# Two-layer hybrid encoder trunk: where the high and low parts of the expert weights are staged

## The chip, the cores and the metric

One NeuronCore of a Trainium2 chip runs the whole program. The time is the device time of one execution in microseconds (us); lower is better. The engines are TensorE (PE; its weight loads are listed as PEld and overlap matmuls), VectorE (DVE), ScalarE (ACT), GpSimd (POOL) and SyncE (SP), which issues the weight transfers. Each engine works through its own instructions in the order written; engines wait for each other on counting semaphores.

## The reference

The input is a sequence of 256 tokens of width 1024 in float32. Layer 0 is an input projection, dilated attention beside an RWKV-7 mixer, an output projection and a dense SwiGLU. Layer 1 is a short convolution beside a gated DeltaNet, and then eight experts of which each token uses two. The change touches only the experts:

```python
def moe_swiglu(h, router, w_gate, w_up, w_down):
    ...
    for e in range(N_EXPERTS):
        out = out + gates[..., e:e + 1] * swiglu(h, w_gate[e], w_up[e], w_down[e])
    return out
```

with `swiglu(h, g, u, d) = (silu(h @ g) * (h @ u)) @ d`, N_EXPERTS = 8, and a hidden width of 3584 per expert.

## The kernel before, in words

**Precision.** A float32 product a*w is made of three products of a faster format: a = a_high + a_low, w = w_high + w_low, and a_high*w_high + a_high*w_low + a_low*w_high is summed in one PSUM bank. `product` (L2844) issues these three matmuls, at L2847, L2848 and L2849. The high part of the weights is a rounded copy made by ScalarE (L1204), the low part is weights minus high part, made by VectorE (L2031).

**Weight halves.** Each expert has 7 chunks of 512 hidden columns. A chunk has a gate, an up and a down part, each cut into two halves of [128, 2048] float32 (1 MB). One expert so has PER = 42 halves, in the order of `expert_chunks`: gate j, up j, then down j-1 (the down part of a chunk comes one chunk late). This text numbers the halves of an expert from 0 to 41, chunk j's gate being 6j-2 and 6j-1, its up 6j and 6j+1, then down j-1 at 6j+2 and 6j+3 (chunk 0, with no down part ahead, has 0 and 1, 2 and 3); down 5 is 38 and 39, down 6 is 40 and 41. Halves of the next expert count on from 42. Where b is used, it is the first gate half of a chunk, b+1 the second.

**Path of a half.** SyncE loads it into the ring (tile `ring`, 7 places of one half, L563). ScalarE waits for the landing and for a free staging, and writes the high part into `split`. VectorE waits for the high part and writes the low part beside it. There are NSTAGE = 3 stagings of one high and one low half each, all in the tile `split`. TensorE waits for the low part (w_lo), does the 12 matmuls of the half and counts half_ps. ScalarE waits for half_ps of half r-3 before it writes the high part of half r. SyncE waits for the low part of half r before it loads half r+7 into the same place (L568, L575, L580).

**Duties.** Between the halves, ScalarE and VectorE also do the other work of the experts. It is written into a table by hand, `duties[r]`, and done at step r, ahead of the part of half r:
- silu of chunk j (ScalarE, L1189), at step g1+3, g1 being the second gate half;
- product of chunk j, silu times up (VectorE, L2015), at step u1+3, u1 being the second up half;
- turned: TensorE transposes the product of chunk j behind the gate halves of chunk j+1 (L2906, `turn`), ScalarE copies the result as a high part (L1192) and VectorE makes the low part (L2019), at step g1+3 of chunk j+1; for chunk 6 at step 41;
- tokens (step 40): TensorE transposes the next expert's tokens behind half 37 (L2872, `turn_rows`), VectorE weighs them (L1984, two operations); tokens_split (step 41): ScalarE (L1170) and VectorE (L1993) split them into high and low;
- result of the expert before (step 2): ScalarE scales its two banks (L1156), when half 41 is done; gates (5), select (6) and rows (10) are small.

At the end of an expert TensorE does: up 6 (halves 36, 37), `turn_rows`, half 38, `turn(6)`, half 39, halves 40 and 41. The last expert has no tokens duties. Expert 0 and expert 7 are written out, experts 1 to 6 are one loop.

**Elsewhere.** The dense stage of layer 0 has the same splitting with the low part written over the ring (L1675). GpSimd moves token rows through HBM: copies of x and of the normalised x in the first expert, then one gather and one scatter with addition per expert (L704, L708).

Of the kernel before, what the change touches and what calls it, by code (L numbers as in the profile page):

```python
# [5 lines left out]
F32 = mybir.dt.float32  # L6
F32R = mybir.dt.float32r
# [4 lines left out]
ADD, SUB, MUL, MAX, MIN = ALU.add, ALU.subtract, ALU.mult, ALU.max, ALU.min  # L12

P = 128
D = 1024
SEQ = 256
TT = SEQ // P
KT = D // P
# [6 lines left out]
NE = 8  # L25
# [8 lines left out]
NSTAT = 3  # L34
HALF = 2048
NHALF = 7
NSTAGE = 3
EC = 512
NC_E = FE // EC
NLEV = 7  # L40
# [57 lines left out]
def hybrid_trunk(nc, A, out):  # L98
# [6 lines left out]
    for i, (kind, n, dmas) in enumerate(chunks):  # L105
        s = (i if i < 8 else i + 2) % NSTAT
# [11 lines left out]
    with ctx:  # L118
        def sb(name, shape, dt=F32):
            return ctx.enter_context(nc.sbuf_tensor(name, shape, dt))  # L120
# [45 lines left out]
        alog_row, dt_row = rows[:, BC_AL:BC_AL + 8], rows[:, BC_DT:BC_DT + 8]  # L166


        with nc.sbuf_tensor("scr", [P, NSTAGE * 2 * HALF + KT * SEQ], F32) as scr:
            pass  # L170
        split = sb("split", [P, NSTAGE * 2 * HALF + KT * SEQ], F32R)
        with nc.sbuf_tensor("ehf", [P, 2 * 2 * 4 * P], F32) as ehf:
            pass
        ehr_ = sb("ehr_", [P, 2 * 2 * 4 * P], F32R)
        wst = split[:, 0:NSTAGE * 2 * HALF].rearrange("p (b t n) -> p b t n", b=NSTAGE, t=2)
        xgs = split[:, NSTAGE * 2 * HALF:NSTAGE * 2 * HALF + KT * SEQ].rearrange("p (t k s) -> p t k s", t=2, k=KT)
        ehs = ehr_[:, :].rearrange("p (b t k s) -> p b t k s", b=2, t=2, k=4)
        hT = scr[:, NSTAGE * 2 * HALF:NSTAGE * 2 * HALF + KT * SEQ].rearrange("p (k s) -> p k s", k=KT)

        B = [ctx.enter_context(nc.psum_tensor(f"bank{i}", [P, 512], F32)) for i in range(8)]  # L180

# [101 lines left out]
        Tc2, Pc2, Xs2 = xn_f[:, 0:512], xn_f[:, 512:1024], xn_f[:, 1024:1152]  # L283
        g_o3 = Region(arena, 6144, 4096)
        INVB = [(Tm, Pm, Xm, Am)] * 4 + [tuple([g_o3.take(4, P) for _ in range(2)] for _ in range(4))] * 2
        g_o4 = Region(scr, SCR0, NSTAGE * 2 * HALF)
        yTo, ktok, vto, osum = g_o4.take(KT, SEQ), g_o4.take(TT, 512), g_o4.take(TT, 512), g_o4.take(TT, 512)
        kkm = [g_o4.take(4, P) for _ in range(TT)]
        kqm = [g_o4.take(4, P) for _ in range(TT)]
# [186 lines left out]
        duties[10].append(("rows", 0))  # L476
        for j in range(NC_E):
            g1, u1 = at_half["gate", j, 1], at_half["up", j, 1]
            duties[g1 + 3].append(("silu", j))
            duties[u1 + 3].append(("product", j))  # L480
            duties[at_half["gate", j + 1, 1] + 3 if j + 1 < NC_E else PER - 1].append(("turned", j))
        duties[PER - 2].append(("tokens", 0))
        duties[PER - 1].append(("tokens_split", 0))

# [11 lines left out]

        def used_half(i, ps, r):

            return i * PER + (NE * PER * ps + NSTAGE + r + 1)

        block = ctx.enter_context(nc.Block())

# [2 lines left out]
        def _(sp):  # L505
# [49 lines left out]
            if UPTO >= 4:  # L555
                packed_w = {"gate": A["od_moe_gate"], "up": A["od_moe_up"], "down": A["od_moe_down"]}

                def expert_load(e, r):

                    kind, j, h = order[r]  # L560
                    v = ring[:, (r % NHALF) * HALF:(r % NHALF + 1) * HALF]
                    src = packed_w[kind][e, 2 * j + h].rearrange("o p n -> p (o n)")
                    sp.dma_start(v, src).then_inc(landed_e[r % NHALF], 16)  # L563

                def expert_pass(ps):
                    for r in range(NHALF):
                        if ps:
                            sp.wait_ge(w_lo, NE * PER * ps - NHALF + r + 1)  # L568
                        elif r < 2 * NSTAT:
                            sp.wait_ge(*used_up(*before[r // 2]))  # L570
                        expert_load(slice(0, 1), r)
                    with sp.Fori(0, NE - 1) as i:
                        for r in range(NHALF, PER + NHALF):

                            sp.wait_ge(w_lo, i * PER + (NE * PER * ps + r - NHALF + 1))  # L575
                            if order[r % PER][1:] == (0, 0):
                                sp.sem_inc(sp_pace, 1)
                            expert_load(bass.ds(i + 1 if r >= PER else i, 1), r % PER)
                    for r in range(NHALF, PER):
                        sp.wait_ge(w_lo, (NE - 1) * PER + NE * PER * ps + r - NHALF + 1)  # L580
                        expert_load(slice(NE - 1, NE), r)

                def store(ps):

                    for q in range(4):
                        c = slice(512 * (q // 2), 512 * (q // 2) + 512)
                        sp.wait_ge(cmb_sb, 4 * ps + 1 + q)
                        sp.dma_start(out[0, P * (q % 2):P * (q % 2) + P, c], x_sb[:, q % 2, c]).then_inc(stored, 16)

                expert_pass(0)  # L590
                store(0)
                sp.wait_ge(flag_rdy, 1)
                with sp.If(sp.value_load(flag[0:1, 0:1], min_val=0, max_val=1) > 0):
                    sp.wait_ge(stored, 64)
                    expert_pass(1)
                    store(1)
                    sp.wait_ge(stored, 128)
                sp.wait_ge(stored, 64)
# [132 lines left out]
        def _(act):  # L731
# [382 lines left out]
            if UPTO >= 4:  # L1114
# [57 lines left out]
                def expert(ps, i, at, last_one=False):  # L1172

                    first = at == 0

                    def duty(what, j):
                        if what == "tokens_split":
                            if not last_one:
                                split_tokens(ps, i, at + 1)
                        elif what == "result":  # L1180
                            if not first:
                                result(ps, i, at)
                        elif what == "gates":
                            if last_one:
                                act.wait_ge(st_ps, ps + 1)
                                act.activation(selT, B[3][:, 0:TT * P], ACT.Copy).then_inc(st_sb, 1)
                        elif what == "silu":
                            act.wait_ge(half_ps, used_half(i, ps, at * PER + at_half["gate", j, 1]))
                            act.activation(esil[:, j % 2, :], B[j % 2][:, :], ACT.Silu).then_inc(eg_act, 1)  # L1189
                        elif what == "turned":  # L1190
                            act.wait_ge(ht_ps, i * NC_E + (NC_E * (at + NE * ps) + 1 + j))
                            act.activation(ehs[:, j % 2, 0], B[6 + j % 2][:, :].rearrange("p (k s) -> p k s", k=4),  # L1192
                                           ACT.Copy).then_inc(ht_hi, 1)

                    for r in range(PER + 1):
                        if first and r == 2:
                            split_tokens(ps, 0, 0)
                        for what, j in duties[r]:
                            duty(what, j)
                        if r < PER:  # L1200
                            act.wait_ge(landed_e[r % NHALF], i * (16 * PER // NHALF) + (
                                16 * PER // NHALF * (at + NE * ps) + 16 * (r // NHALF + 1)))
                            act.wait_ge(half_ps, used_half(i, ps, at * PER + r - NSTAGE))
                            act.activation(wst[:, r % NSTAGE, 0, :], ring[:, (r % NHALF) * HALF:(r % NHALF + 1) * HALF],  # L1204
                                           ACT.Copy).then_inc(w_hi, 1)

                def all_experts(ps):
# [14 lines left out]
        def _(dve):  # L1222
# [679 lines left out]
            if UPTO >= 4:  # L1902
# [92 lines left out]
                def expert(ps, i, at, last_one=False):  # L1995
# [26 lines left out]
                    for r in range(PER + 1):  # L2022
                        if at == 0 and r == 2:
                            weigh_tokens(ps, 0, 0)
                            split_tokens(ps, 0, 0)
                            next_rows(ps, 0, 0)
                        for what, j in duties[r]:
                            duty(what, j)
                        if r < PER:
                            dve.wait_ge(w_hi, i * PER + (PER * (at + NE * ps) + r + 1))  # L2030
                            dve.tensor_tensor(wst[:, r % NSTAGE, 1, :], ring[:, (r % NHALF) * HALF:(r % NHALF + 1) * HALF],  # L2031
                                              wst[:, r % NSTAGE, 0, :].bitcast(F32), SUB).then_inc(w_lo, 1)

                def all_experts(ps):

# [24 lines left out]
        def _(pe):  # L2060
# [769 lines left out]
            if UPTO >= 4:  # L2830

                logits(1).then_inc(pe_step, 1)
                pe.sem_inc(half_ps, NSTAGE)
                unread(512)
                unread(256)
                pe.wait_ge(dve_step, DVE_STEPS["as_rdy"])
# [6 lines left out]

                def product(o, hi, lo, r, cols_, start, stop):  # L2844

                    wh, wl = (wst[:, r % NSTAGE, t, cols_] for t in range(2))
                    pe.matmul(o, hi, wh, start=start, stop=False)  # L2847
                    pe.matmul(o, hi, wl, start=False, stop=False)  # L2848
                    return pe.matmul(o, lo, wh, start=False, stop=stop)  # L2849
# [170 lines left out]
```

## Time and profile before

| | |
|---|---|
| median of 3 runs | 1660.81 us (1660.61 to 1662.0) |
| span of the profiled execution | 1664.3 us |
| TensorE busy | 1636.6 us (98%) |
| VectorE busy | 1229.1 us (74%) |
| ScalarE busy | 986.1 us (59%) |
| expert stage, first to last matmul of a half | 686.3 to 1655.5 us |
| transfers over the span | 440.40 MB, mean 265 GB/s |

The profile is of one execution, by the hardware's profiler. A matmul's duration is longer than the distance to the next one, because they are pipelined; the start times tell how fast TensorE goes. "Idle before" an instruction is time in which its engine did nothing, with what ended it in brackets.

### The profile page before, as it was taken

How to read it: one execution, taken by the hardware profiler on the slowest of the kernel's cores; microseconds unless marked ns; L12 is line 12 of the kernel's file. 1: busy time of each engine (PE TensorE's matmuls, PEld its weight loads, DVE VectorE, ACT ScalarE, POOL GpSimd, SP SyncE). 2: the span in 40 equal slices, each digit the busy share in tenths (PEclk: the TensorE clock that was granted, in tenths of full speed). 3: DMA queues.
4: the chain of work that ended last, by engine and by line, in shares of the span. 5: the costliest groups of instructions: out<-in, count | busy, mean ns of one | idle time of the engine just before them, and what ended most of it. 6: DMA issues, size and time to landing. Idle time of an engine off the chain costs nothing.

```text
span 1664.3 us, 21926 instructions
## 1 busy us (share of the span) xinstructions
PE 1636.6 (98%) x8446; PEld 1343.7 (81%) x8446; DVE 1229.1 (74%) x1203; ACT 986.1 (59%) x955; POOL 101.0 (6%) x122
## 2 busy tenths in 40 slices
PE   8999999999999999999999999999999999999997
PEld 4868995999988886788788788788888888888886
DVE  5578545444424673788888988988888888988886
ACT  3356333434334422677777777777777777777774
POOL 2005230000000030010000000000000000000000
PEclk9999999999999999899999999999999999999999
DMA  6311014455444211899999999999999999999993
GB/s 248 109 62 40 1 52 152 152 198 169 165 153 150 103 51 39 315 421 412 355 375 383 361 381 376 367 382 367 375 376 358 390 371 363 390 367 350 410 375 122
DMA packets 102340, 440.40 MB, mean 265 GB/s; under 512 B 11114, under 2 KB 34942, under 8 KB 59262
## 3 DMA queue, kind: packets, MB, share of 16 engines
q1 hardware_dynamic: 99102, 427.90, 67.7%
q0 software_dynamic: 3168, 11.54, 2.3%
q8 instruction: 48, 0.79, 0.2%
q14 instruction: 22, 0.18, 0.0%
HBM read 431.54 MB, written 7.86 MB: 264 GB/s over the span
## 4 chain that ended last, share of the span: by engine, by line
PE 89%; DVE 6%; ACT 2%; issue 2%; DMA 0%; SPq 0%; DVEq 0%; ACTq 0%
PE bank L2847 16%; PE bank L2849 16%; PE bank L2848 16%; PE bank L2619 5%; PE bank L2549 4%; PE bank L2550 4%; PE bank L2548 4%; DVE split L2031 3%; PE bank L2139 3%; PE bank L2314 2%; PE bank L2782 2%; PE bank L2103 2%; PE bank L2518 2%; PE bank L2337 2%; ACT split L1204 2%
## 5 line engine op out<-in xcount | busy, mean ns | idle before, releaser
L2031 DVE TENSOR_TENSOR split<-ring,split 128x2048 fp32r<-128x2048 f32 x336 | 761.9, 2288 | 115.6 <-ACT split L1204 112.5
L1204 ACT ACTIVATE split<-ring 128x2048 fp32r<-128x2048 f32 x336 | 637.8, 1918 | 165.0 <-PE bank L2849 165.0
L2847 PE MATMUL bank<-split 128*128 128x512 f32 x896 | 354.6, 396 | 2.3 <-DVE split L2031 1.2
L2849 PE MATMUL bank<-split 128*128 128x512 f32 x896 | 349.5, 390 | 0.0
L2848 PE MATMUL bank<-split 128*128 128x512 f32 x896 | 348.9, 389 | 0.0
L2847 PEld LDWEIGHTS bank<-split 128*128 128x128 f32 x896 | 168.3, 188 | 38.9 <-DVE split L2031 4.1
L2849 PEld LDWEIGHTS bank<-split 128*128 128x128 f32 x896 | 168.2, 188 | 35.9
L2848 PEld LDWEIGHTS bank<-split 128*128 128x128 f32 x896 | 168.5, 188 | 32.9
L2847 PE MATMUL bank<-split,ehr_ 128*128 128x512 f32 x448 | 182.7, 408 | 4.4 <-DVE split L2031 4.4
L2849 PE MATMUL bank<-split,ehr_ 128*128 128x512 f32 x448 | 175.9, 393 | 0.0
L2848 PE MATMUL bank<-split,ehr_ 128*128 128x512 f32 x448 | 175.3, 391 | 0.0
L1675 DVE TENSOR_TENSOR ringr<-ring,split 128x2048 fp32r<-128x2048 f32 x33 | 75.3, 2291 | 85.9 <-ACT split L986 85.9
L2549 PE MATMUL bank<-ringr,split 128*128 128x256 f32 (+1 forms) x440 | 134.2, 305 | 0.0
L2847 PEld LDWEIGHTS bank<-split,ehr_ 128*128 128x128 f32 x448 | 84.5, 189 | 34.8 <-DVE split L2031 11.4
L986 ACT ACTIVATE split<-ring 128x2048 fp32r<-128x2048 f32 x33 | 62.9, 1916 | 81.3 <-DMA ring<-in_ev_ffn_up 44.9
L2548 PE MATMUL bank<-ehr_,split 128*128 128x256 f32 x352 | 100.0, 284 | 1.4 <-DVE ringr L1241 1.4
L2849 PEld LDWEIGHTS bank<-split,ehr_ 128*128 128x128 f32 x448 | 84.4, 188 | 18.7
L2550 PE MATMUL bank<-ehr_,ringr 128*128 128x256 f32 x352 | 99.1, 282 | 0.0
L2848 PEld LDWEIGHTS bank<-split,ehr_ 128*128 128x128 f32 x448 | 84.7, 189 | 15.7
L2619 PE MATMUL bank<-scr,ring 128*128 128x256 f32 x384 | 87.9, 383 | 0.3 <-issue 0.3
L2549 PEld LDWEIGHTS bank<-ringr,split 128*128 128x128 f32 x440 | 83.5, 190 | 3.8
L2619 PEld LDWEIGHTS bank<-scr,ring 128*128 128x128 f32 x384 | 71.3, 190 | 9.8 <-ACT scr L797 0.7
(515 smaller groups left out, 1921.9 us busy)
## 6 DMA issues: line engine op xcount, KB each, us to landing
ring<-in_od_moe_gate SPq DMA_DIRECT2D x112, 1024.0 KB, 7.2
ring<-in_od_moe_up SPq DMA_DIRECT2D x112, 1024.0 KB, 7.3
ring<-in_od_moe_down SPq DMA_DIRECT2D x112, 1024.0 KB, 7.2
ring<-in_od_w_in SPq DMA_DIRECT2D x7, 2048.0 KB, 7.6
ring<-in_ev_ffn_gate SPq DMA_DIRECT2D x11, 1024.0 KB, 5.3
ring<-in_ev_ffn_up SPq DMA_DIRECT2D x11, 1024.0 KB, 7.8
ring<-in_ev_w_in SPq DMA_DIRECT2D x5, 2048.0 KB, 9.1
ring<-in_ev_ffn_down SPq DMA_DIRECT2D x5, 2048.0 KB, 7.7
```

Source lines behind the costliest of these rows:

```text
L986: act.activation(homes[q % NHOME], ring[:, v], ACT.Copy).then_inc(pc_hi, 1)
L1204: act.activation(wst[:, r % NSTAGE, 0, :], ring[:, (r % NHALF) * HALF:(r % NHALF + 1) * HALF], ACT.Copy).then_inc(w_hi, 1)
L1675: dve.tensor_tensor(ringr[:, v], ring[:, v], homes[q % NHOME].bitcast(F32), SUB).then_inc(pc_lo, 1)
L2031: dve.tensor_tensor(wst[:, r % NSTAGE, 1, :], ring[:, (r % NHALF) * HALF:(r % NHALF + 1) * HALF], wst[:, r % NSTAGE, 0, :].bitcast(F32), S ...
L2139: last = pe.matmul(B[6 + m % 2][:, SEQ * i:SEQ * i + SEQ], w8[:, k, P * f:P * f + P], hT[:, k, :], start=(k == 0), stop=(k == KT - 1))
L2548: pe.matmul(o, sh, mh, start=start, stop=False, skip_group_check=True)
L2549: pe.matmul(o, sh, ml, start=False, stop=False, skip_group_check=True)
L2550: return pe.matmul(o, sl, mh, start=False, stop=stop, skip_group_check=True)
L2619: last = pe.matmul(B[t % 2][:, SEQ * f:SEQ * f + SEQ], w8[:, k, c:c + P], hT[:, k, :], start=(k == 0), stop=(k == KT - 1))
L2847: pe.matmul(o, hi, wh, start=start, stop=False)
L2848: pe.matmul(o, hi, wl, start=False, stop=False)
L2849: return pe.matmul(o, lo, wh, start=False, stop=stop)
```

## The change

The room of the three pairs of stagings (six halves) is given to six high parts, NHI = 6. The low part of a half is written over the loaded weights in the ring. So a place of the ring is free only when TensorE is done with the half, and SyncE's waits are on half_ps instead of w_lo. The duties silu, product and turned move from three to four halves behind their half; turned of chunk 6 stays at step 41, tokens at 40 and tokens_split at 41. The product of chunk 6 moves from step 40 to step 41.

```diff
-NSTAGE = 3
+NHI = 6
...
-        wst = split[:, 0:NSTAGE * 2 * HALF].rearrange("p (b t n) -> p b t n", b=NSTAGE, t=2)
...
+        w_high = [split[:, HALF * i:HALF * i + HALF] for i in range(NHI)]
+        w_low = [ringr[:, HALF * i:HALF * i + HALF] for i in range(NHALF)]
...
-            duties[g1 + 3].append(("silu", j))
-            duties[u1 + 3].append(("product", j))
-            duties[at_half["gate", j + 1, 1] + 3 if j + 1 < NC_E else PER - 1].append(("turned", j))
+            duties[g1 + 4].append(("silu", j))
+            duties[u1 + 4].append(("product", j))
+            duties[at_half["gate", j + 1, 1] + 4 if j + 1 < NC_E else PER - 1].append(("turned", j))
         duties[PER - 2].append(("tokens", 0))
         duties[PER - 1].append(("tokens_split", 0))
...
-            return i * PER + (NE * PER * ps + NSTAGE + r + 1)
+            return i * PER + (NE * PER * ps + NHI + r + 1)
...
-                            sp.wait_ge(w_lo, NE * PER * ps - NHALF + r + 1)
+                            sp.wait_ge(half_ps, used_half(0, ps, r - NHALF))
...
-                            sp.wait_ge(w_lo, i * PER + (NE * PER * ps + r - NHALF + 1))
+                            sp.wait_ge(half_ps, used_half(i, ps, r - NHALF))
...
-                        sp.wait_ge(w_lo, (NE - 1) * PER + NE * PER * ps + r - NHALF + 1)
+                        sp.wait_ge(half_ps, used_half(NE - 1, ps, r - NHALF))
...
-                            act.wait_ge(half_ps, used_half(i, ps, at * PER + r - NSTAGE))
-                            act.activation(wst[:, r % NSTAGE, 0, :], ring[:, (r % NHALF) * HALF:(r % NHALF + 1) * HALF],
+                            act.wait_ge(half_ps, used_half(i, ps, at * PER + r - NHI))
+                            act.activation(w_high[r % NHI], ring[:, (r % NHALF) * HALF:(r % NHALF + 1) * HALF],
...
-                            dve.tensor_tensor(wst[:, r % NSTAGE, 1, :], ring[:, (r % NHALF) * HALF:(r % NHALF + 1) * HALF],
-                                              wst[:, r % NSTAGE, 0, :].bitcast(F32), SUB).then_inc(w_lo, 1)
+                            dve.tensor_tensor(w_low[r % NHALF], ring[:, (r % NHALF) * HALF:(r % NHALF + 1) * HALF],
+                                              w_high[r % NHI].bitcast(F32), SUB).then_inc(w_lo, 1)
...
-                pe.sem_inc(half_ps, NSTAGE)
+                pe.sem_inc(half_ps, NHI)
...
-                    wh, wl = (wst[:, r % NSTAGE, t, cols_] for t in range(2))
+                    wh, wl = w_high[r % NHI][:, cols_], w_low[r % NHALF][:, cols_]
```

## Rows read from the trace of the kernel before

**Rows 1.** The page: engine shares; groups (busy, mean ns | idle before, releaser).

```profile
PE 1636.6 (98%) x8446; PEld 1343.7 (81%) x8446; DVE 1229.1 (74%) x1203; ACT 986.1 (59%) x955; POOL 101.0 (6%) x122
...
L2031 DVE TENSOR_TENSOR split<-ring,split 128x2048 fp32r<-128x2048 f32 x336 | 761.9, 2288 | 115.6 <-ACT split L1204 112.5
...
L1675 DVE TENSOR_TENSOR ringr<-ring,split 128x2048 fp32r<-128x2048 f32 x33 | 75.3, 2291 | 85.9 <-ACT split L986 85.9
```

**Rows 2.** Waits of PEld, then PE, 690 to 1664 us: total, times, longest.

```profile
PEld bank L2847 <- DVE split L2031: 15.6, 38, 0.8
...
PE bank L2847 <- DVE split L2031: 5.6, 14, 2.2
```

**Rows 3.** Timeline at 1002 us, first half of a down part: start, length, engine, line.

```profile
999.73 4.49 DVE L2031 TENSOR_TENSOR split<-ring,split 128x2048 fp32r<-128x2048 f32 x2 [1.24 <-ACT split L1204]
...
1002.08 0.19 PEld L2847 LDWEIGHTS bank<-split,ehr_ 128*128 128x128 f32 x1 [0.26 <-DVE split L2031]
...
1002.41 0.40 PE L2848 MATMUL bank<-split,ehr_ 128*128 128x512 f32 x1
```

**Rows 4.** Timeline, the same place in the first expert.

```profile
726.38 0.47 PE L2847 MATMUL bank<-split,ehr_ 128*128 128x512 f32 x1
...
726.68 0.39 PE L2848 MATMUL bank<-split,ehr_ 128*128 128x512 f32 x1
```

**Rows 5.** Timeline of TensorE at the passage from expert 3 to 4.

```profile
1150.85 0.60 PE L2906 MATMUL bank<-ident,arena 128*128 128x128 f32 x4
...
1156.75 1.03 PE L2872 MATMUL bank<-ident,arena 128*128 128x128 f32 x8
...
1160.38 0.60 PE L2906 MATMUL bank<-ident,arena 128*128 128x128 f32 x4
...
1166.95 0.50 PE L2847 MATMUL bank<-split,ehr_ 128*128 128x512 f32 x1 [0.32 <-DVE split L2031]
...
1175.63 0.51 PE L2847 MATMUL bank<-split 128*128 128x512 f32 x1 [0.20 <-DVE split L2031]
```

**Rows 6.** The same passage, timelines of ScalarE and VectorE.

```profile
1161.01 0.60 ACT L1192 ACTIVATE ehr_<-bank 128x512 fp32r<-128x512 f32 x1 [2.15 <-PE bank L2906]
...
1162.55 3.71 ACT L1204 ACTIVATE split<-ring 128x2048 fp32r<-128x2048 f32 x2
...
1154.40 4.50 DVE L2031 TENSOR_TENSOR split<-ring,split 128x2048 fp32r<-128x2048 f32 x2 [1.24 <-ACT split L1204]
1158.81 0.68 DVE L2015 TENSOR_TENSOR arena<-bank,arena 128x512 f32<-128x512 f32 x1
1159.41 1.28 DVE L1984 TENSOR_TENSOR arena<-bank,cols 128x512 f32<-128x512 f32 x2
1160.61 2.28 DVE L2031 TENSOR_TENSOR split<-ring,split 128x2048 fp32r<-128x2048 f32 x1
...
1164.61 6.69 DVE L2031 TENSOR_TENSOR split<-ring,split 128x2048 fp32r<-128x2048 f32 x3
```

**Rows 7.** Last expert: TensorE's longest wait; then one microsecond (busy, clock, DMA).

```profile
1648.33 0.47 PE L2847 MATMUL bank<-split,ehr_ 128*128 128x512 f32 x1 [2.17 <-DVE split L2031]
...
1650.00:1651.00 1.00, 1.00 (x4) 0.50 0.06 16
```

**Rows 8.** Loads at L563: issue to landing, 680-700, 710-720, 1000-1150 us.

```profile
DMA to landing us min/median/max: 4.7/4.9/6.5
...
DMA to landing us min/median/max: 10.5/11.5/13.3
...
DMA to landing us min/median/max: 6.3/7.2/10.1
```

**Rows 9.** Two stretches: busy per engine, clock, DMA share, GB/s.

```profile
474.00:482.00 8.00, 5.94 (x34) 4.26 (x33) 4.26 (x10) 4.89 (x11) 0.00 (x0) 1.00 0.98 365
...
724.00:755.00 31.00, 31.00 (x140) 25.22 (x139) 27.72 (x15) 21.82 (x13) 0.00 (x0) 1.00 1.01 423
```

More of the change, by code:

```diff
@@ L166, in hybrid_trunk @@
         alog_row, dt_row = rows[:, BC_AL:BC_AL + 8], rows[:, BC_DT:BC_DT + 8]
-        with nc.sbuf_tensor("scr", [P, NSTAGE * 2 * HALF + KT * SEQ], F32) as scr:
+        with nc.sbuf_tensor("scr", [P, NHI * HALF + KT * SEQ], F32) as scr:
             pass
-        split = sb("split", [P, NSTAGE * 2 * HALF + KT * SEQ], F32R)
+        split = sb("split", [P, NHI * HALF + KT * SEQ], F32R)
         with nc.sbuf_tensor("ehf", [P, 2 * 2 * 4 * P], F32) as ehf:
@@ L174, in hybrid_trunk @@
         ehr_ = sb("ehr_", [P, 2 * 2 * 4 * P], F32R)
-        wst = split[:, 0:NSTAGE * 2 * HALF].rearrange("p (b t n) -> p b t n", b=NSTAGE, t=2)
-        xgs = split[:, NSTAGE * 2 * HALF:NSTAGE * 2 * HALF + KT * SEQ].rearrange("p (t k s) -> p t k s", t=2, k=KT)
+        w_high = [split[:, HALF * i:HALF * i + HALF] for i in range(NHI)]
+        w_low = [ringr[:, HALF * i:HALF * i + HALF] for i in range(NHALF)]
+        xgs = split[:, NHI * HALF:NHI * HALF + KT * SEQ].rearrange("p (t k s) -> p t k s", t=2, k=KT)
         ehs = ehr_[:, :].rearrange("p (b t k s) -> p b t k s", b=2, t=2, k=4)
-        hT = scr[:, NSTAGE * 2 * HALF:NSTAGE * 2 * HALF + KT * SEQ].rearrange("p (k s) -> p k s", k=KT)
+        hT = scr[:, NHI * HALF:NHI * HALF + KT * SEQ].rearrange("p (k s) -> p k s", k=KT)
         B = [ctx.enter_context(nc.psum_tensor(f"bank{i}", [P, 512], F32)) for i in range(8)]
@@ L285, in hybrid_trunk @@
         INVB = [(Tm, Pm, Xm, Am)] * 4 + [tuple([g_o3.take(4, P) for _ in range(2)] for _ in range(4))] * 2
-        g_o4 = Region(scr, SCR0, NSTAGE * 2 * HALF)
+        g_o4 = Region(scr, SCR0, NHI * HALF)
         yTo, ktok, vto, osum = g_o4.take(KT, SEQ), g_o4.take(TT, 512), g_o4.take(TT, 512), g_o4.take(TT, 512)
```

## The prediction

> **What bounds the kernel now.** I read the page first: TensorE is busy in 1636.6 of 1664.3 us [rows 1]. The end of the kernel is therefore set by what TensorE does, and a change that leaves its matmuls alone can only win back its gaps or add new ones. The expert stage runs from 686 to 1656 us and holds 336 weight halves, 42 to an expert, each used by 12 matmuls that start about 0.227 us apart (from the transposes at 1150.85 to those at 1156.75 [rows 5] TensorE does one turn of 0.36 us, its refill and two halves). A half then lasts 2.72 us. VectorE needs 2288 ns for the low part of each [rows 1], ScalarE about 1.9 us for the high part.
>
> Then I read TensorE's waits over the expert stage: before a weight load it waited for VectorE's low part 38 times, 15.6 us in total, and 14 times 5.6 us before a matmul [rows 2]. Part of the 15.6 us only delays a weight load that otherwise runs beneath a matmul, so this is not the gain; the start times tell it. The timeline at 1002 us shows one such wait. The first of two low parts that began at 999.73 ended at about 1002.0, the weight load went at 1002.08, and the second matmul started 0.33 us after the first instead of 0.23 [rows 3]. So a late low part costs TensorE 0.10 to 0.13 us here. It occurs at the first down half of each chunk. The three stagings explain it: ScalarE may write the high part of half r only once TensorE is done with r-3, and behind the two duties of that step (1.1 us together) nothing is left of the lead. In the first and last expert, which stand outside the loop, the same place costs more: at 726.38 a start gap of 0.30 instead of 0.23, and as much ahead of it [rows 4], together with the rest of the half about 0.2 us.
>
> Last I read the passage from one expert to the next, where waits are larger: 0.32 us at 1166.95, 0.20 us at 1175.63 [rows 5].
>
> **The change part by part.** Nothing is removed or added in instructions; the low part is written in place. That costs nothing: the same operation written over the ring, in the dense stage, took 2291 ns against 2288 [rows 1].
>
> *Six high stagings.* ScalarE and VectorE may run further ahead. With duties one half later, high part b+5 follows the silu that waits for half b+1, so inside an expert each low part is ready about 1.0 half (2.7 us) or more before its use. All short waits within experts should go: 4 each in six looped experts at 0.12, 2.9 us; 4 each in the first and last at 0.2, 1.6 us; and about 0.5 us for single late halves at the start of these two. Sum 5.0 us; bounds 0 (the gap belongs to the two waits of a down half, not to the late low part) and 5.6.
>
> *Duties one half later.* Most of them find room. One doesn't. For chunk 6 the product moves from step 40 to step 41, but the tokens duty stays at step 40. VectorE works in order, so the product now stands behind both weighings of the tokens and behind the low part of half 40. Before, it stood ahead of all three: product 1158.81, weighings 1159.41, low part 1160.61 [rows 6]. The transposes of chunk 6 wait for this product, and they started at 1160.38 [rows 5], 0.9 us after it ended. I now put the new order on these rows. The low part of half 39 is the first after the silu, at 1154.40, and ends at 1156.69. The weighings need the token transposes of 1156.75 [rows 5]; four transposes take 0.6 us to reach the reader, so the weighings run from 1157.4, 1.20 us together, to 1158.6. Low part 40 takes until 1160.8 (2.2 us from start to start), the product ends at 1161.5, and the transposes start at 1161.6: **1.2 us late**.
>
> What follows is late as well. ScalarE's turned duty comes 0.63 us behind the transposes (1161.01 against 1160.38), now at 1162.2; high part 41 starts 1.54 us behind it (as 1162.55 behind 1161.01 [rows 6]) at 1163.75 and ends at 1165.65; low part 41 runs 1165.75 to 1168.04, where it began at 1164.61 before. TensorE, from 1161.6 on, has the transposes (0.3 us) and halves 39 and 40 (2.8 us each with their refill) to do, wants half 41 at 1167.55 and gets it at 1168.1. So the old wait of 0.5 us stays, and half 41 starts 1.15 us later than its 1166.95. Half 44 hangs on it through the result duty (it waits for half 41, then high and low part of 44), and starts 8.68 us behind 41 as before (1175.63). No lead can be built across this, since the high part of 41 stands behind the turned duty and that of 44 behind the result. The price is **1.15 us at each of 7 passages, 8.0 us**. The last expert has no tokens duty, so its product ends 8.65 us behind the start of the transposes of chunk 5 (3.55 from 1150.85 to 1154.40, two low parts of 2.2, the product 0.7). TensorE wants it after 8.6 us (0.36, 2.83, 2.72 and 2.72): nothing to win or lose there. The wait of 2.17 us behind it [rows 7] stays.
>
> *Ring given back by TensorE.* Load r+7 now waits for the end of half r instead of its low part, some 1.3 halves later. SyncE's queue holds only loads then, so nothing else stands behind the longer wait. From the end of r to the start of r+7 are 6 halves, 17 us with the transposes; 4.3 us of it go to the high and the low part, so a load may take 12.7 us. From 1000 to 1150 us loads landed after 7.2 us (median), at most 10.1: hidden. In the first expert, beside GpSimd's copies (710 to 720), it was 11.5 with a longest of 13.3 [rows 8]. Issued later, each lands about one load later than before, which leaves the worst ones (half 18 to 21) within 0.5 us of their use. I take 0.5 us of new waits, bounds 0 and 2.
>
> The loads need 6 MB in 16.9 us, 372 GB/s, and the queues moved 423 GB/s for 31 us when they were behind [rows 9]. The Trainium skill, DMA: Bandwidth & Descriptors, section "Where 436 GB/s comes from", says that transfers from HBM are bound at about 358 GB/s. By that the 352 MB of experts would take 984 us, longer than the whole stage, and no TensorE gap could be won or lost; the trace disagrees.
>
> *Sum*: +8.0 - 5.0 + 0.5 = +3.5 us, so the span goes from 1664.3 to 1667.8. The profiled execution's span lies 3.5 us above the median of 1660.81 (runs from 1660.61 to 1662.0); the difference carries over to the median: **1664.3 us**.
>
> **The rivals.**
> *Product not late (faster).* If the weighings or low part 40 get done earlier than I work out, say because the transposes of the tokens are read sooner, the 8.0 us don't arise. It decides at 0.9 us of slack before against 2.1 us of added work in front, which speaks against it. Time 1660.8 - 5.0 = 1655.8.
> *Loads are the floor (no change).* Here both gains and losses are absorbed: the queues are busy nearly all the time (share 1.01 at 423 GB/s [rows 9]), and what TensorE loses at a passage it regains because loads wait there anyway. For it: landing takes 7.2 us though it took 4.9 where few were under way, 680 to 700 [rows 8]. Against: no wait of TensorE ends in a load in [rows 2]. Time 1661, that of before. By the page of the Trainium skill named above this would be the case.
> *Ring too short (slower).* From 12.7 us of landing on, TensorE waits for each load; in the first expert, and if the passages' GpSimd transfers add 3 us to the 10.1 of [rows 8], also there. 2 us in the first expert and 0.5 more at each of 6 passages above my sum: 1669.
> *Clock (slower).* After the idle 2.17 us at 1648.33 the granted clock fell to 0.50 (the 1.2 GHz level) around 1650 us [rows 7], and eight matmuls stood 0.43 apart instead of 0.23, 1.6 us. If the new idle of 1.2 us does this at each passage, 11 us more: 1675. Against: from 474 to 482 TensorE was idle in 2.06 of 8 us and the clock stayed at 1.00 [rows 9].
>
> **How the numbers follow.** Forecast 0.58 (1664.3, own range 1661 to 1667.5), product not late 0.14, loads the floor 0.10, ring too short 0.12, clock 0.06. The range is 1655.5 to 1669: it takes in the faster rival and the short ring, and leaves out the clock. A measurement of this kernel tells 0.2%, 3.3 us, from no change; so 1664.1 is the bound, and the forecast lies on it. Half of its 0.58 counts as slower, with the two slower rivals 0.47; the faster rival and a small edge of the forecast make 0.15; the rest, 0.38, is no change.
>
> **What would show it.** In the profile after: VectorE's product of chunk 6 behind the low part of half 40, and TensorE's transposes waiting for it 1.0 to 1.3 us, 7 times (right), or not at all (the faster rival). Waits for low parts inside experts gone, those of half 41 and 44 still there at 0.3 and 0.2 us. ScalarE waiting for loads instead of TensorE. Waits of TensorE in the first expert at halves 18 to 21 would say the ring is short; a granted clock under 1.00 at a passage, that the clock rival holds. I am wrong if the distance from one passage to the next does not grow by 0.4 to 0.9 us (1.15 less 0.5).

## The result, and the profile after

The changed kernel takes 1682.91 us (median of 4 runs, 1682.55 to 1683.52), the kernel before 1661.4 beside it: a ratio of 1.0123, interval 1.0109 to 1.0137, or 20 us slower (21.5 by the medians, since one of the four runs before is as long as 1666.45). I had forecast 1664.3, slower by 3.5. The profiled execution spans 1681.0 us.

The page of the changed kernel: engine shares, then groups (busy, mean ns | idle before, releaser).

```profile
PE 1646.9 (98%) x8446; PEld 1343.8 (80%) x8446; DVE 1223.9 (73%) x1203; ACT 974.2 (58%) x955; POOL 111.6 (7%) x122
...
L2032 DVE TENSOR_TENSOR ringr<-ring,split 128x2048 fp32r<-128x2048 f32 x336 | 753.2, 2287 | 90.5 <-ACT split L1205 90.3
```

TensorE is as full as in [rows 1], only longer. The low part in place costs what it cost (2287 against 2288 ns). The waits of TensorE from 690 to 1664 us (total, times, longest):

```profile
PE bank L2907 <- DVE arena L2016: 6.8, 7, 1.0
PE bank L2848 <- DVE ringr L2032: 1.9, 7, 0.3
```

The first line is new and is what was forecast, seven waits of the transposes of chunk 6 for the product. It explains 7 of 20 us. Behind this window stands the old wait of the last expert, now 2.12 us at 1666.61. The rest is in no wait. The passage from expert 3 to 4 on TensorE shows it, when it is laid beside [rows 5]:

```profile
1159.15 0.60 PE L2907 MATMUL bank<-ident,arena 128*128 128x128 f32 x4
...
1165.16 1.03 PE L2873 MATMUL bank<-ident,arena 128*128 128x128 f32 x8
...
1169.94 0.66 PE L2907 MATMUL bank<-ident,arena 128*128 128x128 f32 x4 [0.97 <-DVE arena L2016]
...
1176.45 0.50 PE L2848 MATMUL bank<-split,ehr_ 128*128 128x512 f32 x1 [0.27 <-DVE ringr L2032]
```

From the transposes of chunk 5 to those of the tokens, with two halves and no wait between them, it is 6.01 us. In [rows 5] it is 5.90. So 24 matmuls take 0.11 us more. Over all matmuls of the expert stage that follow one another without a wait, the mean distance of their starts is 0.2320 us, against 0.2277 before (the latter with the slower matmuls behind its short waits in it; without them 0.2267). A half takes 2.78 instead of 2.72 us. 336 times 0.05 to 0.06 is 17 to 20 us; with 8 for the product and 5 less for short waits that are gone, this makes the loss. The granted clock is 1.00 in both kernels there, and the slower pace holds from the second half of the first expert (2.79 us; before 2.72) to the last half of the last. In that last half no load is under way and ScalarE and VectorE have a single short operation each:

```profile
1669.25 0.39 PE L2850 MATMUL bank<-split,ehr_ 128*128 128x512 f32 x1
...
1671.81 0.39 PE L2849 MATMUL bank<-ringr,ehr_ 128*128 128x512 f32 x1
1672.04 0.39 PE L2850 MATMUL bank<-split,ehr_ 128*128 128x512 f32 x1
```

That is 12 matmuls in 2.79 us (1669.25 to 1672.04). The same half of the kernel before says nothing, as it lies in and behind a stretch of half clock; in e7, e9 and e13 below it takes 2.72 us. With the other engines this idle, they aren't the cause. The Trainium skill, SBUF — State Buffer, section "Who interferes with whom", says that TensorE never waits for another engine and that transfers don't contend with engines; the trace agrees so far as the pace of this quiet half, 2.79 us, is that of the halves with loads under way, 2.78.

The ring given back later did no harm. Issue to landing, 710 to 720 us and 1000 to 1150 us:

```profile
DMA to landing us min/median/max: 9.9/10.6/11.5
...
DMA to landing us min/median/max: 4.7/6.9/8.3
```

Both are below [rows 8], and no wait of TensorE ends at a late load. ScalarE does wait for loads now, as I had said it would, where it waited for TensorE before (165.0 us in 199 waits; here total, times, longest):

```profile
ACT split L1205 <- DMA ring<-in_od_moe_up: 50.3, 48, 2.7
ACT split L1205 <- DMA ring<-in_od_moe_down: 26.2, 46, 1.6
```

### The profile page after: what moved, and what is told of

The parts are those of the page before. It is cut to its first block, busy times and chain, and to the rows that moved or that the text cites. A ratio compares the mean times of both kernels' runs of the same rounds, so it can differ in the third digit from the quotient of the medians.

```text
span 1681.0 us, 21932 instructions
## 1 busy us (share of the span) xinstructions
PE 1646.9 (98%) x8446; PEld 1343.8 (80%) x8446; DVE 1223.9 (73%) x1203; ACT 974.2 (58%) x955; POOL 111.6 (7%) x122
## 4 chain that ended last, share of the span: by engine, by line
PE 91%; DVE 4%; ACT 3%; issue 1%; DMA 0%; ACTq 0%; DVEq 0%
PE bank L2848 17%; PE bank L2850 17%; PE bank L2849 17%; PE bank L2620 5%; PE bank L2550 4%; PE bank L2551 4%; PE bank L2549 4%; DVE ringr L2032 3%; PE bank L2140 2%; PE bank L2315 2%; PE bank L2783 2%; PE bank L2104 2%; PE bank L2519 2%; PE bank L2338 2%; PE bank L2907 2%; ACT split L1205 2%
## 5 line engine op out<-in xcount | busy, mean ns | idle before, releaser
L2032 DVE TENSOR_TENSOR ringr<-ring,split 128x2048 fp32r<-128x2048 f32 x336 | 753.2, 2287 | 90.5 <-ACT split L1205 90.3
L2848 PE MATMUL bank<-split 128*128 128x512 f32 x896 | 359.7, 401 | 1.6 <-DVE split L1994 1.0
L2850 PE MATMUL bank<-split 128*128 128x512 f32 x896 | 352.7, 394 | 0.0
L2849 PE MATMUL bank<-ringr,split 128*128 128x512 f32 x896 | 351.4, 392 | 0.0
L2850 PEld LDWEIGHTS bank<-split 128*128 128x128 f32 x896 | 168.1, 188 | 41.2
L2848 PEld LDWEIGHTS bank<-split 128*128 128x128 f32 x896 | 168.1, 188 | 40.7 <-DVE ringr L2032 3.2
L2849 PEld LDWEIGHTS bank<-ringr,split 128*128 128x128 f32 x896 | 168.3, 188 | 37.1
L2848 PE MATMUL bank<-split,ehr_ 128*128 128x512 f32 x448 | 179.9, 402 | 4.0 <-DVE ringr L2032 4.0
L2850 PE MATMUL bank<-split,ehr_ 128*128 128x512 f32 x448 | 176.3, 394 | 0.0
L2849 PE MATMUL bank<-ringr,ehr_ 128*128 128x512 f32 x448 | 175.8, 392 | 0.0
L1193 ACT ACTIVATE ehr_<-bank 128x512 fp32r<-128x512 f32 x56 | 33.6, 599 | 184.6 <-PE bank L2907 184.6
L1676 DVE TENSOR_TENSOR ringr<-ring,split 128x2048 fp32r<-128x2048 f32 x33 | 75.3, 2292 | 85.9 <-ACT split L987 85.9
L2848 PEld LDWEIGHTS bank<-split,ehr_ 128*128 128x128 f32 x448 | 84.0, 188 | 25.7 <-DVE ringr L2032 5.0
L2850 PEld LDWEIGHTS bank<-split,ehr_ 128*128 128x128 f32 x448 | 84.1, 188 | 20.4
L2849 PEld LDWEIGHTS bank<-ringr,ehr_ 128*128 128x128 f32 x448 | 84.1, 188 | 18.4
L2550 PEld LDWEIGHTS bank<-ringr,split 128*128 128x128 f32 x440 | 83.4, 190 | 3.8
```

Source lines behind the costliest of these rows:

```text
L1676: dve.tensor_tensor(ringr[:, v], ring[:, v], homes[q % NHOME].bitcast(F32), SUB).then_inc(pc_lo, 1)
L2032: dve.tensor_tensor(w_low[r % NHALF], ring[:, (r % NHALF) * HALF:(r % NHALF + 1) * HALF], w_high[r % NHI].bitcast(F32), SUB).then_inc(w_lo, 1)
L2550: pe.matmul(o, sh, ml, start=False, stop=False, skip_group_check=True)
```

## The experiments

Theories of the slow pace: **A**, it hangs on where the low part lies that TensorE reads; **B**, on what happens in the ring or on the new waits. The mean distances of starts (690 to 1650 us) in the table below are worked out from the timeline of TensorE. The second column has how many bytes apart the first high and the first low part lie (with the low part in the ring, the distance of other pairs differs from this by multiples of 8192). The third has what is left over when it is divided by 256.

| kernel | high and low part | distance mod 256 | start to start, us | ratio to before |
|---|---|---|---|---|
| before | 8192 apart | 0 | 0.2277 | 1 |
| changed | 143712 | 96 | 0.2320 | 1.0123 |
| e1 | high read twice | 0 | 0.2273 | 1.0027 |
| e2 | 3 stagings, low in ring | 96 | 0.2321 | 1.0074 |
| e4 | 57344 | 0 | 0.2273 | 1.0043 |
| e5 | 143744 | 128 | 0.2321 | 1.0125 |
| e6 | 57376 | 32 | 0.2313 | 1.0100 |
| e9 | 57344 | 0 | 0.2276 | 1.0031 |
| e10 | 145408 | 0 | 0.2275 | 1.0038 |
| e11 | 143872 | 0 | 0.2275 | 1.0034 |
| e12 | before, 8224 apart | 32 | 0.2328 | 1.0086 |
| e13 | 144128 | 0 | 0.2274 | 1.0035 |

Of the others, e3 is placed as the changed kernel (0.2320), e7 and e8 as e4 (0.2273, 0.2271), e14 as before (0.2277).

**e1_middle_reads_high.** The middle matmul reads the high part again, so the product with the low part of the weights is left out of the sum.

```diff
-                    wh, wl = w_high[r % NHI][:, cols_], w_low[r % NHALF][:, cols_]
+                    wh, wl = w_high[r % NHI][:, cols_], w_high[r % NHI][:, cols_]
```

> The changed kernel, but the middle of the three matmuls reads the high part of the weights a second time instead of the low part in the ring (so the low product of the weights is left out; all else, the writing of the low part and the waits on it too, stays). In the changed kernel matmuls of the experts start 0.232 us apart, before 0.227; 4032 of them make 20 us. Theory A, the pace hangs on where the low part that TensorE reads lies: the pace goes back to 0.227 and the time falls by 18 to 22 us to 1661 to 1665. Theory B, the pace hangs on what the other engines and transfers do in the ring (in-place writes, loads), or on the new waits: 0.232 stays, and 1683.

Measured 1666.22 us, ratio 1.0027 (1.0014 to 1.0039), pace 0.2273. The in-place writes, loads and waits are all still there; B falls, A stands. The time is 1 us above what A gave.

**e2_only_low_over_ring.** The kernel before with the low part in the ring.

```diff
-                            dve.tensor_tensor(wst[:, r % NSTAGE, 1, :], ring[...
+                            dve.tensor_tensor(ringr[:, (r % NHALF) * HALF:(r % NHALF + 1) * HALF], ring[...
...
-                    wh, wl = (wst[:, r % NSTAGE, t, cols_] for t in range(2))
+                    wh = wst[:, r % NSTAGE, 0, cols_]
+                    wl = ringr[:, (r % NHALF) * HALF:(r % NHALF + 1) * HALF][:, cols_]
```

with SyncE's waits on half_ps as in the change.

> The kernel before, with one part of the change alone: the low part is written over the loaded half and read there, and the ring is given back by TensorE; three stagings, the duties and ScalarE's waits as before. Theory A (place of the low part): pace 0.232, so 20 us slower than before, 1679 to 1683. Theory B' (the slower pace comes from six stagings or the later duties): pace 0.227 and the time of before within 3 us.

Measured 1676.37 us, ratio 1.0074 (1.0042 to 1.0106), pace 0.2321. The pace comes with the low part alone; stagings and duties have no part in it. The time is 3 us less than expected: with longer halves the late low parts inside a looped expert no longer hold TensorE (the starts at the first down halves, 0.33 us in [rows 3], are regular here), so an expert takes 122.30 us, 1.5 more than before.

**e3_product_first.** The product of chunk 6 back ahead of the tokens.

```diff
-            duties[u1 + 4].append(("product", j))
+            duties[u1 + (4 if j + 1 < NC_E else 3)].append(("product", j))
```

> The changed kernel with the product of chunk 6 back at step 40, ahead of the tokens duty. If my working of the passages holds, TensorE's waits for this product (6.8 us over 7 passages by the trace of the change) vanish and the low part of half 41 comes about 1.1 us earlier: 7 to 8 us less than the changed kernel, 1675 to 1676. If half 41 is held by something else, the waits move there and less than 2 us are won.

Measured 1675.56 us, ratio 1.0080 (1.0051 to 1.0109), 7.3 us less than the changed kernel. The waits for the product are gone, and half 41 follows the transposes of the tokens by 10.11 us instead of 11.29:

```profile
1162.06 1.03 PE L2873 MATMUL bank<-ident,arena 128*128 128x128 f32 x8
1165.71 0.60 PE L2907 MATMUL bank<-ident,arena 128*128 128x128 f32 x4
1172.17 0.51 PE L2848 MATMUL bank<-split,ehr_ 128*128 128x512 f32 x1 [0.27 <-DVE ringr L2032]
```

**e4_ring_beside_split.** The ring's tile is allocated directly ahead of the high parts.

```diff
-        with nc.sbuf_tensor("ring", [P, NHALF * HALF], F32) as ring:
-            pass
-        ringr = sb("ringr", [P, NHALF * HALF], F32R)
         x_sb = sb("x_sb", [P, TT, D])
...
+        with nc.sbuf_tensor("ring", [P, NHALF * HALF], F32) as ring:
+            pass
+        ringr = sb("ringr", [P, NHALF * HALF], F32R)
         with nc.sbuf_tensor("scr", [P, NHI * HALF + KT * SEQ], F32) as scr:
```

> The changed kernel, with the ring's tile allocated directly ahead of the tile of the high parts instead of at the front of the memory; nothing else changes. The distance of low and high parts shrinks, and both tiles then have the same address modulo 64 bytes, which they don't have in the changed kernel (16512 and 160224). Theory A1 (distance or alignment of the two addresses decides): pace 0.227, 1661 to 1665. Theory A2 (reading a second tile as such, wherever it lies, costs): 0.232 and 1683.

Measured 1667.79 us, ratio 1.0043 (1.0031 to 1.0055), pace 0.2273. Two halves and their transposes take 5.91 us again, and the passage's waits stand alone:

```profile
1150.44 0.60 PE L2907 MATMUL bank<-ident,arena 128*128 128x128 f32 x4
...
1156.35 1.03 PE L2873 MATMUL bank<-ident,arena 128*128 128x128 f32 x8
...
1161.13 0.66 PE L2907 MATMUL bank<-ident,arena 128*128 128x128 f32 x4 [1.00 <-DVE arena L2016]
...
1167.65 0.50 PE L2848 MATMUL bank<-split,ehr_ 128*128 128x512 f32 x1 [0.40 <-DVE ringr L2032]
```

The time is 3 us above what A1 gave. A2, reading a second tile as such, falls; the addresses decide. Distance and alignment had both changed, and the next runs part them.

**e5_pad_far** and **e6_pad_beside.** 32 bytes ahead of the high parts, with the ring at the front (e5) or beside them (e6).

```diff
+        sb("pad", [P, 8])
         with nc.sbuf_tensor("scr", [P, NHI * HALF + KT * SEQ], F32) as scr:
```

> The changed kernel with an unused tile of 32 bytes ahead of the tile of the high parts: that tile moves from 160224 to 160256, the ring stays at 16512. Both addresses are then multiples of 64 bytes, and as far apart as in the changed kernel. Theory C (it matters that high and low parts, read in turn, have the same address modulo 64): pace 0.227, 1666 to 1669. Theory D (the distance matters, or reading the ring's low part at a multiple of 64): pace 0.232, 1683.

> The ring beside the tile of the high parts, as in the run that brought the pace back, but with the unused 32 bytes between them: ring at 102880 (32 modulo 64), high parts at 160256 (0 modulo 64). Theory C: pace 0.232, 1681 to 1684. Theory D (distance): pace 0.227, 1666 to 1669.

Measured 1683.74 (1.0125, 1.0104 to 1.0147) and 1679.55 us (1.0100, 1.0077 to 1.0124), paces 0.2321 and 0.2313. Both are slow. C, the same address modulo 64, falls by e5; D's distance falls by e6. Two readings were left: the difference of the addresses must be a multiple of something above 128 (**E**), or an address that is a multiple of 64 is slow (**F**).

**e9_both_shifted**, **e10_far_pad1696**, **e11_far_pad160.** e9 has the 32 bytes ahead of the ring and the high parts together; e10 and e11 are e5 with 1696 and 160 bytes.

```diff
-        sb("pad", [P, 8])
+        sb("pad", [P, 424])
```

> The ring beside the high parts as in the fast run, and 32 unused bytes ahead of both: 102912 and 160256. Both are now multiples of 64 and still 57344 = 7 x 8192 bytes apart. Theory E (the pace hangs on high and low parts lying a multiple of some size over 128 bytes apart): pace 0.227, 1666 to 1669. Theory F (reading at a multiple of 64 bytes costs, in all slow kernels so far at least one address is one): pace 0.232, 1682.

> The changed kernel with 1696 unused bytes ahead of the high parts: ring at 16512, high parts at 161920, 145408 = 71 x 2048 bytes apart, both multiples of 64. Theory E, if its size is 2048 or less: pace 0.227, 1666 to 1669. Theory E with a larger size, or theory F: 0.232, 1683.

> The same with 160 unused bytes: the distance is 143872 = 281 x 512 bytes, and not a multiple of 1024. Theory E with a size of 256 or 512: pace 0.227, 1666 to 1669. Theory E with 1024 or 2048: 0.232, 1683, or a pace between.

Measured 1667.73 (1.0031, 1.0011 to 1.0051), 1668.69 (1.0038, 1.0024 to 1.0051) and 1668.93 us (1.0034, 1.0020 to 1.0047), all at the fast pace. F falls, as all three read at multiples of 64. E stands, with 256 or 512 bytes.

**e12_before_low_shifted.** The kernel before, each low part moved by 32 bytes.

```diff
-        wst = split[:, 0:NSTAGE * 2 * HALF].rearrange("p (b t n) -> p b t n", b=NSTAGE, t=2)
+        ST = 2 * HALF + 8
+        w_high = [split[:, ST * i:ST * i + HALF] for i in range(NSTAGE)]
+        w_low = [split[:, ST * i + HALF + 8:ST * i + ST] for i in range(NSTAGE)]
```

> The kernel before (three stagings of high and low part side by side in one tile), with 32 unused bytes between each high and its low part, so that they lie 8224 instead of 8192 bytes apart. Theory E (the distance must be a multiple of 256 or 512 bytes): pace 0.232 instead of 0.227, 16 to 20 us slower than before, 1678 to 1682. Theory G (the slow pace belongs to low parts read from the ring, and the paddings helped in another way): pace 0.227 and 1661.

Measured 1677.4 us, ratio 1.0086 (1.0062 to 1.0110), pace 0.2328. Nothing of the change is in this kernel, the ring is only loaded and read by ScalarE and VectorE, and the pace is slow. The same two events as above lie 6.02 us apart:

```profile
1155.32 0.60 PE L2908 MATMUL bank<-ident,arena 128*128 128x128 f32 x4
...
1161.34 1.04 PE L2874 MATMUL bank<-ident,arena 128*128 128x128 f32 x8
```

**e13_far_pad416.** e5 with 416 bytes, 144128 = 563 x 256.

```diff
-        sb("pad", [P, 8])
+        sb("pad", [P, 104])
```

> The changed kernel with 416 unused bytes ahead of the high parts: high and low parts lie 144128 bytes apart, a multiple of 256 and not of 512. Theory E with 256: pace 0.227, 1667 to 1669. Theory E with 512: 0.232, 1683. I expect the second a little more, since 384 bytes over a multiple of 512 was slow.

Measured 1668.26 us, ratio 1.0035 (1.0023 to 1.0046), pace 0.2274. I leaned to the other side; 256 is enough, and 128 (e5) isn't.

**A second stage, in every kernel.** The down product of the dense stage (323 to 474 us) also reads high parts from `split` and low parts from the ring, with 512 columns. Neither its code nor its waits belong to the change. Its first 48 matmuls start at the first line and end where the second starts, here before and then in e4:

```profile
323.03 0.39 PE L2548 MATMUL bank<-split 128*128 128x512 f32 x1
...
334.19 0.28 PE L2548 MATMUL bank<-ehr_,split 128*128 128x256 f32 x1
...
321.30 0.40 PE L2549 MATMUL bank<-split 128*128 128x512 f32 x1
...
332.21 0.28 PE L2549 MATMUL bank<-ehr_,split 128*128 128x256 f32 x1
```

They take 11.16 and 10.91 us. Over the stage the distance is 0.2314 us before, in the changed kernel, e1, e3 and e14 (the distance is 96 modulo 256 in all of them), 0.2319 to 0.2324 in e5, e6 and e12, and 0.2272 in e4, e7 to e11 and e13. The products of 256 columns in the same stage go the other way: there the moving operands are the tokens (`ehr_` and the ring), and they start 0.1200 us apart in the kernels that are fast with 512 columns and 0.1178 before and in the changed one. So the stage as a whole takes 186.5 us in e4, e10 and e13 against 185.3 in e3 and e14, 1.2 longer.

**e7_beside_product_first.** e3 and e4 together.

> The changed kernel with both repairs: ring beside the high parts, and the product of chunk 6 at step 40 ahead of the tokens duty. Measured singly they gave 15 and 7.4 us. If they add, 1660 to 1661, against 1661 of the kernel before: 5 us of waits within experts won by the change, and 3 to 4 us given to something that I can't name yet. If the product's delay and the pace hide each other, 1664 or more.

Measured 1659.5 us, ratio 0.9981 (0.9970 to 0.9991). The repairs add. What is left of the change is a gain of 3 us by the medians. The waits for half 41 and 44 are as before:

```profile
1154.55 1.03 PE L2873 MATMUL bank<-ident,arena 128*128 128x128 f32 x8
1158.17 0.60 PE L2907 MATMUL bank<-ident,arena 128*128 128x128 f32 x4
1164.63 0.50 PE L2848 MATMUL bank<-split,ehr_ 128*128 128x512 f32 x1 [0.40 <-DVE ringr L2032]
1173.30 0.51 PE L2848 MATMUL bank<-split 128*128 128x512 f32 x1 [0.20 <-DVE ringr L2032]
```

**e8_late_duties.** e7 with three duties moved behind the weight parts.

```diff
-        duties[2].append(("result", 0))
+        duties[4].append(("result", 0))
...
-        duties[PER - 1].append(("tokens_split", 0))
+        duties[PER].append(("turned_late", NC_E - 1))
+        duties[PER].append(("tokens_split", 0))
...
-                        elif what == "turned":
-                            act.wait_ge(ht_ps...
+                        elif what == "turned_late" or what == "turned" and j < NC_E - 1:
+                            act.wait_ge(ht_ps...
...
-                        elif what == "turned":
-                            dve.wait_ge(ht_hi...
+                        elif what == ("turned_late" if last_one and j == NC_E - 1 else "turned"):
+                            dve.wait_ge(ht_hi...
```

> The same, and three duties moved so that no part of a half stands behind them at the passages: ScalarE's result duty from step 2 to step 4, its turned duty of chunk 6 behind the high part of half 41 (in the last expert VectorE's too), tokens_split on both engines behind half 41. By my working of the passages the waits for half 41 and 44 (0.5 and 0.35 us, 7 times) go, and in the last expert the wait of 2.1 us with the clock drop behind it (1.6 us): 9 to 10 us below the kernel with both repairs, 1650 to 1652, 0.6% below the kernel before. If half 41 is held by VectorE's own work, only the last expert's 3.5 us are won: 1657.

Measured 1648.34 us (1644.7 to 1649.46), ratio 0.9915 (0.9898 to 0.9931), faster than both kernels and 2 us below what I expected. VectorE at the passage has the low part of half 41 (1152.31) ahead of the tokens' split, and runs five low parts in a row behind it:

```profile
1147.01 0.69 DVE L2017 TENSOR_TENSOR arena<-bank,arena 128x512 f32<-128x512 f32 x1 [0.26 <-PE bank L2851]
1147.62 1.28 DVE L1986 TENSOR_TENSOR arena<-bank,cols 128x512 f32<-128x512 f32 x2
1148.82 2.28 DVE L2033 TENSOR_TENSOR ringr<-ring,split 128x2048 fp32r<-128x2048 f32 x1
1151.70 0.69 DVE L2021 TENSOR_TENSOR ehr_<-bank,ehr_ 128x512 fp32r<-128x512 f32 x1 [0.61 <-ACT ehr_ L1194]
1152.31 2.28 DVE L2033 TENSOR_TENSOR ringr<-ring,split 128x2048 fp32r<-128x2048 f32 x1
1154.51 1.28 DVE L1995 TENSOR_TENSOR split<-arena,split 128x512 fp32r<-128x512 f32 x2
1155.72 11.09 DVE L2033 TENSOR_TENSOR ringr<-ring,split 128x2048 fp32r<-128x2048 f32 x5
```

Of TensorE's waits from 690 us on, one is left, in the combination at the end:

```profile
PE bank L2885 <- DVE arenar L1958: 1.1, 1, 1.1
```

**e14_before_late_duties.** The kernel before with these duties, without the change.

> The kernel before with the later duties alone: result at step 4, turned of chunk 6 behind the high part of half 41 (in the last expert VectorE's too), tokens_split behind half 41; stagings, ring and the other duties as before. With three stagings the high part of half 41 may start when TensorE is done with half 38, at about the time of the turned duty, so little of the passage's waits should go: 0.3 us at each of 7 passages, and 1.5 to 3.5 us at the end of the last expert, 1655 to 1660. Theory H (the duties were what held the kernel, six stagings add nothing): 1650 to 1652, as the repaired changed kernel with the same duties.

Measured 1658.14 us, ratio 0.9966 (0.9954 to 0.9979), 0.8 us per expert won where I had given it 0.3. So the duties alone are worth 0.34%, and with six stagings the same duties reach 0.85%; H, by which the duties alone held the kernel, falls.

## Why the prediction was wrong, point by point

**The step that failed** is the first one of the part by part working: "Nothing is removed or added in instructions; the low part is written in place. That costs nothing". I checked it for the engine that writes the low part and not for the one that reads it. I took from the kernel before that a half costs TensorE 2.72 us, as if this were a property of the matmul. It is one of the two addresses too: with high and low part a multiple of 256 bytes apart, 0.227 us, otherwise 0.232. Five placings at a multiple of 256 are fast and four others slow, e12 without any part of the change. From passage to passage it is 123.43 us in the changed kernel and 121.36 in e4, 2.07 us per expert and 16.6 us over eight; less the 1.2 us by which e4 is slower in the dense stage this is 15.4, and the medians give 15.1 (1682.91 less 1667.79). No rival of mine had this mechanism, but the trace of before could have shown its size. I took from the dense stage what the operation over the ring costs VectorE, 2291 ns, and didn't look at the matmuls that read its result there: with the same two tiles at the same addresses they start 0.2314 us apart, against 0.2267 in the experts. That times 4032 is 19 us, 2% of the largest term of all.

My own sign of being wrong came true: from one passage to the next it was to grow by 0.4 to 0.9 us, and it grew by 2.60 (123.43 against 120.83), the product's 1.15 less some 0.6 for waits that are gone, and 2.07 for the pace.

**Product of chunk 6 behind tokens and low part 40: right.** Forecast 1.2 us late at the transposes. They follow those of the tokens by 4.78 us in the changed kernel and in e4, against 3.63 in [rows 5], 1.15 late. VectorE's order is as worked out, with the weighings at 1165.80, the low part at 1167.01 and the product at 1169.20:

```profile
1165.80 1.29 DVE L1985 TENSOR_TENSOR arena<-bank,cols 128x512 f32<-128x512 f32 x2 [0.80 <-PE bank L2873]
1167.01 2.28 DVE L2032 TENSOR_TENSOR ringr<-ring,split 128x2048 fp32r<-128x2048 f32 x1
1169.20 0.69 DVE L2016 TENSOR_TENSOR arena<-bank,arena 128x512 f32<-128x512 f32 x1
```

Half 41 starts 11.30 us behind the tokens' transposes in e4 and 10.20 in [rows 5], 1.1 us later where 1.15 was forecast, and the waits for halves 41 and 44 stayed, as said. Seven of these are 7.7 us; e3 gave 7.3 back.

**Waits within experts: right.** None is left inside an expert. A looped expert of e7 takes 120.14 us, before it was 120.83: 0.7 us won where I had 0.5.

**The sum without the pace: right in the expert stage.** e4, e9, e10, e11 and e13 are the changed kernel at the fast pace. Their ratios are 1.0031 to 1.0043, in the mean 1.0036, or 6.0 us, where the sum said 3.5. In the profiled executions the experts, from the first to the last matmul of a half, take 968.97 us before and 971.46, 972.43 and 972.47 in e4, e10 and e11, which have the same half clock at the end: 3.2 more in the mean. From one passage to the next it is 0.53 us more in e4, within my 0.4 to 0.9. Another 1.2 of the 6.0 us are those of the dense stage, which the sum didn't have. The last 1.6 I can't place. Going from span to median I also made a mistake: the time of an execution is about 2.1 us above its span, so the profiled one of before must be that of 1666.45, 5 us above the others of its kernel, and not one of about 1661.

**Loads, ring: the rivals did not come.** Landings were shorter than before. Theory "loads are the floor" fell by e8: it moves the same bytes in 14 us less, and its expert stage of 950.6 us is shorter than the 984 us that I worked out for 358 GB/s.

**Clock: no fall at the passages, and luck at the end.** The granted clock stayed at 1.00 through the new waits of 1 us. Behind the wait of some 2.1 us in the last expert (1.8 in e14) it fell to 0.50 in eight of the fifteen profiled executions that have this wait (before, e3, e4, e5, e6, e10, e11, e14), for about eight matmuls or 1.6 us, and not in the other seven, the changed kernel among them. My sum took it as there before and after.

**The rival of a product that isn't late** came true only as e7. It gave 3 us by the medians, where I had put 5.

## What to carry to other kernels

When an operand moves to another place, ask of every engine that reads it, and first of the one that sets the time, whether its pace was measured with the old place; if two operands are read in turn by TensorE, with 512 columns keep them a multiple of 256 bytes apart (with 256 columns the dense stage here was slower so), and look at the start-to-start time of a steady stretch. If the kernel already does the same thing in another stage, as the dense stage did here, read there what it costs every engine. With an order of duties written by hand, a shift by one step changes who stands behind whom only where a duty doesn't shift with the others: look there. More buffers give lead only as far as no duty that waits for TensorE stands ahead of the next weight part.

## What the runs showed of the hardware

Matmuls of 512 columns that alternate between two moving operands in SBUF started 0.227 us apart if the addresses differ by a multiple of 256 bytes (8192, 57344, 143872, 144128, 145408) and 0.231 to 0.233 us if they don't (8224, 57376, 143712, 143744). Left over from a multiple of 256 were 32, 96 and 128; no other value was tried. The size isn't set by this alone: 32 gave 0.2313 in e6 and 0.2328 in e12. In the changed kernel all three matmuls of a product are slower, not only the one with the other operand: from high to low part, from low to high, and on to the next product it is 0.2337, 0.2312 and 0.2313 us, in e4 0.2276, 0.2270 and 0.2274. In e6 the first is nearly fast, with 0.2286, 0.2334 and 0.2319. Where the addresses lie otherwise (32 or 0 modulo 64, one tile or two, near or far) made no difference. Matmuls of 256 columns in the dense stage were slower in the placings that are fast with 512, 0.1200 against 0.1178 us.

Behind a wait or a turn the fast pace comes back late: in e7 the second to sixth starts are 0.229 to 0.234 us apart and from the seventh on they are 0.227, some 0.03 us in all.

What inside TensorE does this no run tells. The address of the weight operand alone doesn't decide, as it is the same in the changed kernel, in e1 and in e4. Whether its distance from the moving operands takes part is open.
